# The end of a recurrent mixer taken by chunks and by halves of the tokens, with weight units loaded and split at other places

## The reference

```
y = wkv7_scan(r_h, decay, k_h, v_h, -kk, kk * a_h)        # 256 tokens, 16 heads of 64
mean = jnp.mean(y, -1, keepdims=True)                     # over the 64 values of a head
var = jnp.mean(jnp.square(y - mean), -1, keepdims=True)
y = ((y - mean) * lax.rsqrt(var + GN_EPS)).reshape(B, S, D)
y = y * ln_w + ln_b
bonus = jnp.sum(r_h * k_h * r_k, -1, keepdims=True) * v_h
y = y + bonus.reshape(B, S, D)
return (y * g) @ w_o                                      # w_o is 1024 x 1024, h = h + this
```

## Time and profile before

| | |
|---|---|
| time, median of 3 runs | 1942.72 us (1939.32 to 1943.7) |
| time of the profiled execution | 1941.93 us, span in the trace 1940.0 us |
| PE busy | 1798.1 us (93%) |
| DVE, ACT, POOL busy | 1041.6, 873.7, 1075.5 us |
| mean granted TensorE clock | 0.962 of full |

### The profile page before, as it was taken

The page is one execution under the profiler, slowest core; times in us unless marked ns, Lnnn a source line. Parts: engine busy times, 40 slices in busy tenths (PEclk is TensorE's granted clock), DMA queues, the critical chain, the costliest instruction groups (busy, mean ns, idle before and its releaser), DMA issues. The chain is left out here.

```text
span 1940.0 us, 35805 instructions
## 1 busy us (share of the span) xinstructions
PE 1798.1 (93%) x14142; PEld 1635.1 (84%) x14142; DVE 1041.6 (54%) x1735; ACT 873.7 (45%) x1141; POOL 1075.5 (55%) x409
## 2 busy tenths in 40 slices
PE   7799778999999999999999999899968999679997
PEld 6588668999999999888888878799958689669997
DVE  5953441695457787444444433444365853555343
ACT  4247324445533333445554455555434732245443
POOL 7775547588866666455455566465547200446552
PEclk9899889999999999999999999999989899779999
DMA  7433334255544444566676624345424110224541
GB/s 288 152 131 131 108 130 174 91 183 182 176 154 140 139 141 141 163 194 192 191 246 236 216 98 174 142 184 195 179 94 161 66 24 4 111 109 174 192 177 76
DMA packets 63937, 293.71 MB, mean 151 GB/s; under 512 B 10848, under 2 KB 11232, under 8 KB 45408
## 3 DMA queue, kind: packets, MB, share of 16 engines
q1 hardware_dynamic: 63840, 292.32, 43.9%
HBM read 290.19 MB, written 1.05 MB: 150 GB/s over the span
## 5 line engine op out<-in xcount | busy, mean ns | idle before, releaser
L2299 POOL TENSOR_TENSOR unit_lo<-unit_raw,unit_hi 128x2048 fp32r<-128x2048 f32 x72 | 342.8, 4782 | 236.7 <-ACT unit_hi L1261 236.7
L2308 POOL TENSOR_TENSOR rows_lo<-rows_raw,rows_hi 128x1024 fp32r<-128x1024 f32 x128 | 307.8, 2406 | 136.8 <-ACT rows_hi L1365 85.3
L2316 POOL TENSOR_TENSOR a_lo<-table,a_hi 128x256 fp32r<-128x256 f32 x128 | 176.1, 1376 | 177.6 <-ACT a_hi L1389 177.6
L1964 DVE TENSOR_TENSOR rows_lo<-rows_raw,rows_hi 128x1024 fp32r<-128x1024 f32 x128 | 157.3, 1229 | 191.0 <-ACT rows_hi L1384 191.0
L642 PE MATMUL bank<-x_hi,rows_hi 128*128 128x256 f32 x1024 | 256.2, 288 | 1.7 <-ACT rows_hi L1347 1.7
L643 PE MATMUL bank<-x_lo,rows_hi 128*128 128x256 f32 x1024 | 250.7, 283 | 0.0
L1384 ACT ACTIVATE rows_hi<-rows_raw 128x1024 fp32r<-128x1024 f32 x128 | 135.7, 1060 | 173.2 <-PE bank L704 173.2
L2329 POOL TENSOR_TENSOR up_lo<-up_raw,up_hi 128x2048 fp32r<-128x2048 f32 x22 | 113.5, 5165 | 160.4 <-ACT up_hi L1438 160.4
L1261 ACT ACTIVATE unit_hi<-unit_raw 128x2048 fp32r<-128x2048 f32 x72 | 136.8, 1911 | 140.9 <-PE bank L464 96.4
L642 PEld LDWEIGHTS bank<-x_hi,rows_hi 128*128 128x128 f32 x1024 | 195.8, 191 | 1.9 <-issue 1.9
L643 PEld LDWEIGHTS bank<-x_lo,rows_hi 128*128 128x128 f32 x1024 | 196.1, 192 | 0.0
(11 more groups left out here) (401 smaller groups left out, 3903.4 us busy)
## 6 DMA issues: line engine op xcount, KB each, us to landing
unit_raw<-in_ring SPq DMA_DIRECT2D x77, 1024.0 KB, 4.9
rows_raw<-in_u SPq DMA_DIRECT2D x128, 512.0 KB, 3.5
rows_raw<-in_v SPq DMA_DIRECT2D x128, 512.0 KB, 3.5
up_raw<-in_up SPq DMA_DIRECT2D x44, 1024.0 KB, 6.1
down_raw<-in_down SPq DMA_DIRECT2D x22, 1024.0 KB, 5.4
const<-in_const SPq DMA_DIRECT2D x1, 1792.0 KB, 15.7
X<-in_x SPq DMA_DIRECT2D x2, 512.0 KB, 4.0
vst<-XN SPq DMA_DIRECT2D x8, 128.0 KB, 2.5
```

The lines of the kernel that those rows point to most:

```text
L1964: V.tensor_tensor(rows_lo[q][:, :], rows_raw[q][:, :], rows_hi_f[q % 2], ALU.subtract).then_inc(S("v_lo_ready"), 1)
L2299: nc.gpsimd.tensor_tensor(unit_lo[SLOT_OF[n]][:, :], unit_raw[SLOT_OF[n]][:, :], unit_hi[h % HI_SLOTS][:, :].bitcast(F32), ALU.subtract).t ...
L2308: nc.gpsimd.tensor_tensor(rows_lo[q][:, :], rows_raw[q][:, :], rows_hi_f[q % 2], ALU.subtract).then_inc(S("u_lo_ready"), 1)
L2316: nc.gpsimd.tensor_tensor(a_lo[q % 2][:, :], table[:, t, :], a_hi_f[q % 2], ALU.subtract).then_inc(S("a_lo_ready"), 1)
```

## The change

In the code of the recurrent mixer:

- **Memory.** The tiles of the chunks lie elsewhere: chunk 0 over `unit_hi2` and raw slot 4, chunk 1 over `unit_hi0` and `unit_hi1`, chunks 2 and 3 in the arena and in XN. The scratch (`lane_at`) lies over raw slots 0 to 3. The hi part of the last WO unit has its own place, `last_hi`.
- **Loads.** SP loads the first three WO units once the state-free part of chunk 2 is made (`tt`), the fourth once the outputs of chunk 0 are.
- **Splitting.** ACT rounds the WO units between its copies for the recurrence; POOL subtracts each in four pieces of 128x512, two units behind chunk 0's rows, one behind chunk 2's and one behind chunk 3's.
- **State.** `step_state` adds in PSUM and then multiplies out of PSUM; before, it added into SBUF and multiplied there.
- **Group norm.** Variance, root, scaling and shift go chunk by chunk, inside the recurrence. For chunk 3, DVE sums and centres straight out of PSUM and ACT squares.
- **Output.** Two halves of the tokens (`th`): transposition by 64 products of 64x64 with the identity in two banks, gate multiplied in PSUM, `yg_hi` by ACT and `yg_lo` by DVE from there, then both column halves of w_o for these 128 tokens (`out_rows`). The number of 128x512 products stays 96.

```diff
@@ memory
-    chunk_at = [RING_AT + 3584 * c for c in range(NRC)]
+    MX_AT, SG_AT = ARENA_AT + 2048, ARENA_AT + 2048 * 9
+    pair_at = [HI_AT + 4096, HI_AT, MX_AT, XN_AT]
+    token_at = [raw_at[4], HI_AT + 2048, MX_AT + 2048, XN_AT + 2048]
+    lane_at = [[raw_at[0] + 512 * i for i in range(4)] + [SG_AT, SG_AT + 512], [raw_at[1] + 512 * i for i in range(6)],
+               [raw_at[1] + 3072 + 512 * i for i in range(6)]]
+    last_hi = view("last_hi", MX_AT, [UNIT_W], F32R)
@@ PE
-            for p in range(PAIRS):
-                pe.wait_ge(S("ys_ready"), 2 * p // PAIRS + 3)
-                o = fill(("yt", p))
-                for c in range(NRC):
-                    t = nc.tensor.transpose(o[0:DK, c * P:(c + 1) * P], ys[:, c, p, :], ident)
-                full(("yt", p), t)
-            for j in range(2):
-                rows("wo2", UNIT_AT["WO"] + 2 * j, j, yg_hi, yg_lo, arrived=None if j else yg_arrived)
+            def turned(th):
+                pe.wait_ge(S("ys_ready"), 2 * th + 2)
+                for b in range(2):
+                    o = fill(("yt", th, b), 2)
...
+                                ends[par] = mm(o[r, at_:at_ + RCH], ys[r, 2 * th + half, 4 * b + j, :], ident[r, r], start=True, stop=True)
+                    full_by_heads(("yt", th, b), ends)
+            def out_rows(j, c):
+                o = fill(("wo2", j, c))
+                for half in range(2):
...
+                    wait_hi()
+                    pe.wait_ge(S("yg_hi_ready"), 2 * c + half + 1)
+                    for k in range(4):
+                        mm(o[:, :], tokens(yg_hi, k), hi[:, k, :], start=half == 0 and k == 0, stop=False)
+                    wait_drained(pe, ("yt", c, half))
+                    for k in range(4):
+                        mm(o[:, :], tokens(yg_lo, k), hi[:, k, :], start=False, stop=False)
+                    wait_lo()
+                    for k in range(4):
+                        t = mm(o[:, :], tokens(yg_hi, k), lo[:, k, :], start=False, stop=half == 1 and k == 3)
...
+            for th in range(2):
+                turned(th)
+                for j in range(2):
+                    out_rows(j, th)
@@ SP
+                wait_filled(sp, ("tt", NRC - 2))
+                for n in range(UNIT_AT["WO"], N_UNITS - 1):
+                    load(n)
+                wait_filled(sp, ("y_", 0))
+                load(N_UNITS - 1)
                 wait_filled(sp, ("y_", NRC - 1))
-                for n in range(UNIT_AT["WO"], N_UNITS):
-                    load(n)
@@ ACT
+            def rows_deviation(c):
+                act.wait_ge(S("ys_ms"), c + 1)
+                at_ = 128 + PAIRS * c
+                A(stat[:, at_:at_ + PAIRS], stat[:, at_:at_ + PAIRS], ACT.Sqrt).then_inc(S("ys_sd"), 1)
...
+            yg_hi_of(0)
+            wait_drained(act, ("y_", NRC - 1))
+            A(ysq[:, NRC - 1, :, :], ys[:, NRC - 1, :, :], ACT.Square).then_inc(S("last_squared"), 1)
+            rows_deviation(NRC - 1)
+            yg_hi_of(1)
@@ DVE
-                new = st[(c + 1) % 2][:, :, :]
-                drain(("ds", c), V.tensor_tensor(new, eight(o), st[c % 2][:, :, :], ALU.add))
-                wait_drained(ve, ("ds", c))
-                V.tensor_tensor(new, new, bc(dec_end[:, :, c:c + 1], [PAIRS, DK]), ALU.mult).then_inc(S("state_ready"), 1)
+                step(V.tensor_tensor(o, o, st[c % 2][:, :, :], ALU.add))
+                drain(("ds", c), V.tensor_tensor(st[(c + 1) % 2][:, :, :], o, bc(dec_end[:, :, c:c + 1], [PAIRS, DK]), ALU.mult))
...
+            def rows_scaled(c):
+                ve.wait_ge(S("ys_sd"), c + 1)
+                step(V.reciprocal(each(96, c), each(128, c)))
+                ve.wait_ge(S("rows_shift_ready"), c + 1)
+                y = ys[:, c, :, :]
+                step(V.tensor_tensor(y, y, bc(each(96, c).unsqueeze(2), [PAIRS, DK]), ALU.mult))
+                V.tensor_tensor(y, y, vst[:, c, :, :], ALU.add).then_inc(S("ys_ready"), 1)
@@ POOL
+                    pieces = 4 if n >= UNIT_AT["WO"] else 1
...
-            units_lo(N_UNITS)
+                if c != 1:
+                    units_lo(UNIT_AT["WO"] + (2, 0, 3, 4)[c])
```

More of the change, by code:

```diff
@@ new lines, in out_rows @@
+            def out_rows(j, c):
+                o = fill(("wo2", j, c))
+                for half in range(2):
+                    n = UNIT_AT["WO"] + 2 * j + half
+                    hi, lo, wait_hi, wait_lo = parts(n, 4)
+                    tokens = lambda x, k: x[:, 4 * half + k, c * P:(c + 1) * P]
+                    wait_hi()
[8 more added lines that the diff above has]
+                        t = mm(o[:, :], tokens(yg_hi, k), lo[:, k, :], start=False, stop=half == 1 and k == 3)
+                    if half:
+                        full(("wo2", j, c), t)
+                    elif c == TC - 1:
+                        t.then_inc(S("first_half_done"), 1)
+                        halves_done[0] += 1
+                        release[n] = (S("first_half_done"), halves_done[0])
+                if c == TC - 1:
+                    release_when_filled(n, ("wo2", j, c))
@@ L2207, in _ @@
             step_copy(1, "rhs", rhs8)
+            rows_mean(0)
             k_with_both(c)
@@ L2245, in _ @@
-            step.sync()
-            early, late = slice(0, NRC - 1), slice(NRC - 1, NRC)
-            rows_variance(early)
-            rows_scaled(early, 1)
-            c = NRC - 1
-            rows_mean(c)
-            ve.wait_ge(S("rows_mean_ready"), NRC)
-            step(V.tensor_tensor(ys[:, c, :, :], ys[:, c, :, :], bc(each(64, c).unsqueeze(2), [PAIRS, DK]), ALU.subtract))
-            step(V.tensor_tensor(ysq[:, c, :, :], ys[:, c, :, :], ys[:, c, :, :], ALU.mult))
-            step(V.tensor_reduce(each(96, c), ysq[:, c, :, :], AX, ALU.add))
@@ L2256, in _, with yg_of @@
-            rows_variance(late)
-            step.mark(V.tensor_tensor(ys[:, c, :, :], ys[:, c, :, :], ln_w[:, :, :], ALU.mult))
-            rows_scaled(late, 2)
+            step_copy(c, "rhs", rhs8)
+            rows_scaled(1)
+            step_copy(c, "u", u8)
+            rows_squares(2)
+            def yg_of(th):
+                for b in range(2):
+                    o = wait_filled(ve, ("yt", th, b))[:, :].rearrange("p (j t) -> p j t", j=4)
+                    V.tensor_tensor(o, o, gT[:, 4 * b:4 * b + 4, th * P:(th + 1) * P], ALU.mult).then_inc(S("yg_ready"), 1)
@@ L2259, in _, with yg_lo_of @@
+            def yg_lo_of(th):
+                for b in range(2):
+                    ve.wait_ge(S("yg_hi_ready"), 2 * th + b + 1)
+                    w = (slice(None), slice(4 * b, 4 * b + 4), slice(th * P, (th + 1) * P))
+                    o = PS[plan.at[("yt", th, b)][0]][:, :].rearrange("p (j t) -> p j t", j=4)
+                    drain(("yt", th, b), V.tensor_tensor(yg_lo[w], o, yg_hi[w].bitcast(F32), ALU.subtract))
             for b in range(4):
                 wait_drained(ve, ("g2", b))
-            def yg_lo_of(p):
-                ve.wait_ge(S("yg_hi_ready"), p + 1)
-                V.tensor_tensor(yg_lo[:, p, :], ygT[:, p, :], yg_hi[:, p, :].bitcast(F32), ALU.subtract).then_inc(S("yg_lo_ready"), 1)
@@ L2276, in _ @@
-            yg_lo_of(PAIRS - 1)
+            o = eight(wait_filled(ve, ("y_", c)))
+            step(V.tensor_reduce(each(64, c), o, AX, ALU.add))
+            step(V.tensor_scalar(each(64, c), each(64, c), 1.0 / DK, None, ALU.mult))
+            yg_of(0)
+            drain(("y_", c), V.tensor_tensor(ys[:, c, :, :], o, bc(each(64, c).unsqueeze(2), [PAIRS, DK]), ALU.subtract))
+            rows_variance(c, (S("last_squared"), 1))
+            step.mark(V.tensor_tensor(ys[:, c, :, :], ys[:, c, :, :], ln_w[:, :, :], ALU.mult))
@@ L2277, in _ @@
+            yg_lo_of(0)
+            rows_scaled(2)
+            step.sync()
+            rows_scaled(c)
+            yg_of(1)
+            yg_lo_of(1)
             add_to_x("wo2")
```

103 lines of the change are left out of this document (42 added, 61 removed).

## The result

The change took 1926.51 us (median of 5 runs, 1922.71 to 1929.74) against 1942.65 us (5 runs) of the kernel before: a ratio of 0.9919, 95% interval 0.9903 to 0.9935. Forecast were 1923 us and 1917 to 1930.

A forecast was written before the change was run, and what follows sets the result against it. PE was taken as the bound, with three holes and a lower clock between 1671.43 and 1729.81. Ending the output product at 1710.5 saves 19.3 us: 1941.93 − 19.3 = 1922.6, plus 0.8 for the median, forecast 1923, range 1917 to 1930.

The forecast's parts named there:

- The saving: From PE's gapless recurrence to the output product's end: end moves from 1729.81 to 1710.5, 19.3 us saved.
- The first hole: 3.98 us of PE ahead of the last `u`; `rhs` copied 3.1 us earlier, last group ends 1676.9, gain 5 us.
- the moved loads: w_o loaded and split during the recurrence: 28 us for a load of some 8, priced at 0, range end 3.
- The restart: From the last outputs at 1676.9 to the first `yg_lo` at 1683.8, with PE doing four products before it.
- The clock: PE idles about 0.6 and 3.2 us before 1683.8; fall to the lower clock taken, priced at 3.4 us.
- The rival without a fall: PE's clock stays up in the output stage: 1920 us, or 1918 if meetings cost nothing too; chance 15%.
- The sentence on transposes: Transposes don't count as PE activity for the clock gate; ordinary products with the identity would, favouring no fall.
- From restart to end: Output stage from 1683.8: products, turning and hand-overs 23.3 us to 1707.1, plus 3.4 for the clock, to 1710.5.
- A late engine: Chunk 3's scaling or POOL's last unit comes after PE asks, DVE and POOL blocking each other: 1927 to 1933; 18%.
- The range: 1917 to 1930 us, leaving out low clock throughout, slower, and the far end of the late engine.
- the case that was given 58%: The forecast itself, 1921 to 1926 us.
- the three holes: PE waits of 3.98 us ahead of the last `u`, 12.34 ahead of the transposes, 3.94 ahead of the second product pair.

The follow-up runs named there:

- Paced loads: The change with each w_o unit loaded in four parts of 256 KB, one at a time, each behind another bank of the recurrence: 1923.33 us.
- copies beside the old kernel: The kernel before with four extra 1 MB memory-to-memory copies at the moments the change loads w_o: 1950.55 us.
- the last three runs: The change with paced 256 KB loads and first `yg_lo` early, plus last-unit products late (1919.23 us), also no short TENSOR_SCALARs (1918.47), or without late products but whole POOL units (1919.51).
- three experiments with the same loads: The change without short TENSOR_SCALARs (1927.09 us), with the first `yg_lo` ahead of chunk 3's variance (1927.28), or with both halves turned before any product (1934.39).
- `yg_lo` early: The change with the first half's `yg_lo` made ahead of chunk 3's variance and product by ln_w: 1927.28 us.
- turned together: The change with both halves of the tokens turned before any output product: 1934.39 us.
- pieces undone: The change with POOL subtracting each w_o unit in one 128x2048 instruction again: 1928.56 us.

## Why the prediction was right, and where a step of it failed

- **The saving.** Forecast 19.3 us, measured 16.1 (1729.81 to 1713.70). The rest of the span is the same, 210.2 and 210.0 us, as priced.
- **The first hole and the copies: right in size.** From the end of PE's last `rhs` group to the end of the last outputs 5.5 us were forecast, 5.28 measured. The 3.98 us became 1.06. The copy of `rhs` came 0.27 us after its group, not 0.05, since chunk 2's TENSOR_SCALAR of 0.84 us stood ahead until 1674.93: sum and mean took 1.56 us where 0.93 were priced. The forecast end, 111.6 us after the start of the recurrence, is what the kernel before reaches with the copy moved and no loads (110.8).
- **The step that failed: the moved loads, which the sum has at nothing.** The prediction asked whether w_o is there in time ("28 us for a load of some 8"), not what 3 MB at once do to others. The last `rhs` group ended at 1674.57 instead of 1671.43, 3.1 us late (3.4 from the start of the recurrence on), which is the two holes of 1.30 and 1.94. They come from late instruction packets. Paced loads took back 1.7 us of stage, and copies beside the old kernel cost 8 us. The cost was in no sum and in no rival.
- **The restart.** Last outputs to first `yg_lo` product: 6.9 us forecast, 7.9 measured. ln_w took 1.82 us where 1.29 were priced, and the TENSOR_SCALARs of 128x8 for chunk 3 took 0.72 and 0.35, priced at about 0.17 from chunk 3's row before; one of 1.05 for chunk 2 kept the sum of chunk 3 waiting until 1680.24, 0.39 us after the last outputs. DVE's timeline of the kernel before shows such long ones:

```profile
1668.91 0.53 DVE L2143 TENSOR_SCALAR stat<-stat 128x8 f32<-128x8 f32 x1
...
1670.96 0.94 DVE L2143 TENSOR_SCALAR stat<-stat 128x8 f32<-128x8 f32 x1
```

  Taking the short ones away gave 1.2 us back.
- **The clock.** It fell, as forecast, after the wait of 3.42 us. Priced at 3.4; the three groups of four from 1687.76 on took 1.88, 1.70 and 1.13 between starts where 0.907 is one at the higher clock, which is 2.0 us. The rival without a fall is out for the change, and is what the last three runs show. The sentence on transposes that the prediction takes from the Trainium skill for this rival is not borne out here, and the trace of the kernel before bears on it: PE stood still for 12.34 us and then ran nothing but the 32 transposes until 1699.74, and within them the granted clock went from 0.50 to 1.00. The measurement decides.

```profile
1694.20:1697.20 3.00, 3.00 (x15) 2.50 (x16) 2.42 (x7) 2.54 (x4) 2.56 (x1) 0.50 0.56 235
1697.20:1698.20 1.00, 1.00 (x7) 0.86 (x6) 1.00 (x1) 0.38 (x1) 1.00 (x1) 0.58 0.00 0
1698.20:1699.70 1.50, 1.50 (x15) 1.26 (x12) 1.50 (x2) 0.00 (x0) 1.50 (x2) 1.00 0.00 0
```

- **From restart to end:** 26.7 us forecast, 25.9 measured. The clock cost 1.4 less than priced, the hand-overs and the turning 0.6 more.
- **A late engine:** PE waited neither for `unit_lo` nor for `ys`, as forecast with "Some 4 us of cover" less the meetings. There were 2.7 us (1696.14 to 1698.85), and `yg_lo` early used them up at once.
- **The range** held since no error was large and two have the other sign: +3.1, −0.2, +1.0 and −0.8 make 3.1 of the 3.2 us between 19.3 and 16.1. The median, 1926.51, lies just above the 1921 to 1926 of the case that was given 58%. There was luck in it: in the profiled execution the holes of the recurrence did not bring the lower clock, while in three experiments with the same loads they did, and the recurrence was 2.0 to 3.7 us longer than in the change.
- **What the argument left out and the number hid:** the three holes are told side by side, as if each could be gained. Alone the first gains nothing, since POOL's chain of centring stood behind it; the third alone gives 7 us, with four pieces and no other edit.

## What to carry to other kernels

Price a moved load twice: whether it lands in time, and what runs beside it, since a burst of 1 MB transfers beside many small PE instructions opened holes of 1.3 to 3.7 us that no semaphore explains; spaced parts of 256 KB brought them under 1 us. When such a hole lies in the middle of a group, look at when the instruction packets start. Ask of each hole whether it is on the path by tracing what the next hole waits for, and after closing a wait look for the engine that was 2 or 3 us behind it. Cut an instruction that blocks another engine where someone waits for the blocked one, and leave it whole elsewhere.

## What the runs showed of the hardware that was not expected

- Large transfers, even from memory to memory, delay PE's instruction packets and open holes in the middle of a group: 3.71 us beside 3 MB of copies, 1.30 to 2.11 beside 3 MB of loads, up to 0.64 beside parts of 256 KB, none in the kernel before between 1565 and 1671.
- The length of an idle piece alone does not say whether the clock falls: after 1.84 us in the recurrence it was at 0.50, after 1.94 in the change (1651.26) it stayed at 1.00.

```profile
1653.00:1657.00 4.00, 4.00 (x145) 4.00 (x142) 1.44 (x3) 0.60 (x1) 3.92 (x4) 1.00 0.01 4
```

- Beside POOL a TENSOR_SCALAR of 128x8 in SBUF takes up to 1.29 us (turned together), and 2.01 beside a whole unit (pieces undone), against 0.17 alone. It ends with POOL's instruction: in the change the one of 1.05 us ended at 1680.32 and POOL's instruction beside it at 1680.29, and those of 1.29 and 2.01 us ended as closely behind POOL's (1676.39 and 1676.36; 1659.51 and 1659.49). A RECIPROCAL of the same size stays at 0.19. The two in the change:

```profile
L2195 DVE TENSOR_SCALAR stat<-stat 128x8 f32<-128x8 f32 x4 | 2.1, 534 | 0.1
...
L2202 DVE RECIPROCAL stat<-stat 128x8 f32<-128x8 f32 x4 | 0.8, 188 | 0.0
```

- The two hold each other back: POOL's four pieces beside DVE's scalings took 6.81 us, one whole instruction of the same work 5.05.
